# Two transformer stacks in one kernel: split activations moved to 448 bytes past a multiple of 512, one odd matmul in six stages, and three reorderings

## The chip, the cores and the metric

One Trainium2 chip, one of its cores. The time is the device time of one execution in microseconds (us). Five engines run side by side, each through its own list of instructions, and meet at semaphores: TensorE (PE: matmuls; PEld is its weight load), VectorE (DVE), ScalarE (ACT), GpSimd (POOL) and SyncE (SP, here the queue of the weight transfers).

## The reference

Input x is 256 tokens of 1024 features. It goes through an MLA layer and an mLSTM layer, each with a squared-ReLU MLP, then through a second stack: SwiGLU, short convolution, SwiGLU, and after a shared key/value projection SwiGLU, a sparse attention, SwiGLU. Cut to what the change touches:

```python
def rms_norm(x, g):
    y = x * lax.rsqrt(jnp.mean(x * x, axis=-1, keepdims=True) + EPS)
    return y * g

# MLA: 16 heads, 64 + 32 query/key features, 64 value features
cq = rms_norm(h @ w_dq, q_norm)
q = (cq @ w_uq).reshape(b, s, 16, 96)
dkv = h @ w_dkv
ckv = rms_norm(dkv[..., :256], kv_norm)
kv = (ckv @ w_ukv).reshape(b, s, 16, 64 + 64)
q, k = rms_norm(q, q_gain), rms_norm(k, k_gain)      # then rope on the last 32
o = softmax(q @ k.T * 96 ** -0.5, chunk mask) @ v
# mLSTM: 4 heads of 128 / 256, one row of decays per head
den = sum(qk); h = num / max(abs(den), exp(-m))
# MLPs and SwiGLU
x + square(relu(rms_norm(x, g) @ w1)) @ w2
x + (silu(gate) * up) @ w_out
```

## The kernel before

All matmuls of weights are made in three passes for precision. A weight tile `raw` of 128x1024 (512 KB) comes in by DMA into a ring of four; ScalarE rounds it to `w_hi` (`split`, L538), and VectorE or GpSimd subtracts to get the rest, `w_lo` (`take_lo`, L1006 on VectorE, L462 on GpSimd; `POOL_TILES` says which tiles GpSimd takes). Activations are split in the same way into a high and a low half that lie side by side: `xs` holds the layer's input, `os` attention outputs and the input of glu_2, `hs` the hidden features. A product of 128 features of weights with 256 tokens is then three matmuls of 256 columns: w_hi with x_hi, w_hi with x_lo, w_lo with x_hi (`narrow_product`, L1692, L1693, L1694). The `residual` stages, which read `hs`, use one matmul of 512 columns and one of 256. `token_major` stages (uk, uq, uv, mv, mo, kv, nq) hold the activations still and stream 512 columns of weights (L1820 to L1822).

`STAGES` is the order of the stages: name, tiles, outputs. Long stages that read `xs`: up_0 and up_1 (32 tiles each), glu_0, glu_1, glu_3 (44 each), cin (24). A tile of them is 24 matmuls. `feature` runs them: the first two tiles in pairs, with the row sums of the norm (`sums`) among the last of their products, then tile by tile, the last multiple of eight in a loop; `between` puts other work behind a tile.

Where things lie: each partition has `os` from byte 114112 (448 past a multiple of 512), `xs` from 130720 (160 past) and `hs` from 147104 (160 past). `bias` later takes the place of `os`, `w1c_all` that of `xs`, the `arena` that of `hs`. In the changed kernel `xs` and `w1c_all` begin at 130496 (448 past); the others stay.

Nothing is scheduled by a program: each engine's order is the order in which its part of the code is written. Of those orders the change touches four places:

- The start. ScalarE makes the high halves of x, splits tile 0, then squares x with splits 1 and 2 behind three squares each; VectorE makes the low halves, adds the squares into `ssq` (L1641) and takes the low tiles at the same places. TensorE warms up with 16 matmuls of ones, then runs tile 0, tile 1 (`sums` behind it), tile 2 of dq.
- MLA's projections. dkv and kr follow, and the latents go to `os` split (L1029 the low halves). `narrow` copies kr's output to `fsum` (L1048) for two transposes (`turn_narrow`) that stand behind the first half tile of uk. `sums("cq")` adds 5 blocks of squares for each of 2 token blocks (L1703) behind the second half tile. VectorE then evacuates uk, uq and uv (`up_kv`, L1234), each bank when its tiles are done; TensorE may start uq only when the first two banks of uk are read.
- MLA's heads. Per head: transposes, scores, maxima on VectorE, `exps` on ScalarE with `accum_out` for the row sums (L700), transposes of the probabilities, values (L1901 to L1903) and a scaling by the reciprocal of the sum.
- mLSTM. VectorE makes the decays by a scan, an add, a second scan (L1320 to L1322) behind the eight mqk outputs; TensorE turns the rows behind the third half tile of mv (`turn_rows`), and the scores, weights and numerators of the four heads follow between the half tiles of mv and mo. `head(h)` (L1364 to L1371) divides the numerators by the denominators.

## Time and profile before

| | us |
|---|---|
| median of 3 runs | 1621.61 |
| the runs | 1624.91, 1621.61, 1619.29 |
| profiled execution | 1625.26 |
| its span (first to last instruction) | 1623.4 |
| mean granted clock of TensorE | 0.986 of 2.4 GHz |

The profile is that of one execution. Busy times of matmuls overlap and their ends are modelled, so pace is read from starts or from counts in a stretch, to one matmul in either direction. A granted clock of 1.00 is 2.4 GHz, 0.50 is 1.2 GHz. "Idle before" and a wait tell how long an engine stood and what it waited for.

### The profile page before, as it was taken

The page shows a single profiled execution, that of the slowest core. Times are in us where ns is not written, and L with a number is a line of the kernel's source. Part 1 is how long each engine was busy: PE and PEld are TensorE (multiplying, and loading weights), DVE is VectorE, ACT ScalarE, POOL GpSimd, SP SyncE. Part 2 cuts the span into 40 slices and gives each one's busy share as a digit, 9 for nine tenths or more (in the row PEclk, how much of TensorE's full clock was granted, in tenths as well). Part 3 has the DMA queues.
Part 4 walks back from the last instruction along what each step waited for, and adds up shares of the span by engine and source line. Part 5 has one row for each costly group of instructions (what it writes and reads, how often), then busy time and mean ns, then how long its engine had stood idle before and what let it go on. Part 6 is the DMA issues. An engine that isn't in the chain of part 4 may idle for free.

```text
span 1623.4 us, 33219 instructions
## 1 busy us (share of the span) xinstructions
PE 1585.5 (98%) x11604; PEld 1492.1 (92%) x11604; DVE 1076.5 (66%) x1817; ACT 863.8 (53%) x1381; POOL 151.3 (9%) x133
## 2 busy tenths in 40 slices
PE   7899999999999999999999999999999999999999
PEld 6789998877999889999899999889999878999997
DVE  6668766645677666666787766678566755686665
ACT  5576554444765545445545545556455546664443
POOL 1650000075200000000000000000000032200000
PEclk8899999989999999999999999999999999999999
DMA  6226556543565565555655655556555871065564
GB/s 227 73 56 192 193 182 193 183 155 117 168 190 186 182 196 188 185 183 192 204 188 182 197 189 188 188 181 207 179 190 193 216 198 65 2 195 189 186 195 142
DMA packets 80766, 280.72 MB, mean 173 GB/s; under 512 B 8880, under 2 KB 12464, under 8 KB 80688
## 3 DMA queue, kind: packets, MB, share of 16 engines
q1 hardware_dynamic: 76800, 274.78, 52.5%
q10 hardware_dynamic: 3888, 4.85, 1.6%
q8 instruction: 54, 0.88, 0.2%
q14 instruction: 24, 0.20, 0.0%
HBM read 278.03 MB, written 1.57 MB: 172 GB/s over the span
## 4 chain that ended last, share of the span: by engine, by line
PE 90%; DVE 5%; ACT 2%; DMA 2%; issue 1%; DVEq 0%; ACTq 0%; SPq 0%
PE psum L1692 17%; PE psum L1693 17%; PE psum L1694 17%; PE psum L1684 16%; PE psum L1685 8%; PE psum L1820 2%; PE psum L1822 2%; PE psum L1821 2%; DMA raw<-tiles 1%; DVE w_lo L1006 1%; PE psum L2095 1%; PE psum L2046 1%; PE psum L1994 1%; ACT w_hi L538 1%; DVE w1c_all L1570 0%
## 5 line engine op out<-in xcount | busy, mean ns | idle before, releaser
L538 ACT ACTIVATE w_hi<-raw 128x1024 fp32r<-128x1024 f32 x518 | 546.8, 1057 | 447.9 <-PE psum L1694 263.2
L1006 DVE TENSOR_TENSOR w_lo<-raw,w_hi 128x1024 fp32r<-128x1024 f32 x472 | 577.0, 1223 | 219.6 <-ACT w_hi L538 219.2
L1692 PE MATMUL psum<-xs,w_hi 128*128 128x256 f32 x1928 | 541.6, 281 | 8.5 <-DVE w_lo L1006 5.8
L1694 PE MATMUL psum<-xs,w_lo 128*128 128x256 f32 x1928 | 539.9, 280 | 0.0
L1693 PE MATMUL psum<-xs,w_hi 128*128 128x256 f32 x1928 | 538.9, 279 | 0.0
L1684 PE MATMUL psum<-hs,w_hi 128*128 128x512 f32 x1216 | 421.9, 390 | 0.0
L1692 PEld LDWEIGHTS psum<-xs,w_hi 128*128 128x128 f32 x1928 | 363.5, 189 | 9.5 <-DVE w_lo L1006 6.2
L1693 PEld LDWEIGHTS psum<-xs,w_hi 128*128 128x128 f32 x1928 | 363.5, 189 | 0.3
L1694 PEld LDWEIGHTS psum<-xs,w_lo 128*128 128x128 f32 x1928 | 363.4, 188 | 0.0
L1685 PE MATMUL psum<-hs,w_lo 128*128 128x256 f32 x1216 | 342.9, 282 | 0.0
L1684 PEld LDWEIGHTS psum<-hs,w_hi 128*128 128x128 f32 x1216 | 228.3, 188 | 47.7
L1685 PEld LDWEIGHTS psum<-hs,w_lo 128*128 128x128 f32 x1216 | 229.8, 189 | 0.0
L462 POOL TENSOR_TENSOR w_lo<-raw,w_hi 128x1024 fp32r<-128x1024 f32 x46 | 110.8, 2419 | 1223.9 <-ACT w_hi L538 1191.5
L1692 PE MATMUL psum<-os,w_hi 128*128 128x256 f32 x544 | 152.9, 281 | 1.1 <-DVE os L1200 1.1
L1693 PE MATMUL psum<-os,w_hi 128*128 128x256 f32 x544 | 151.1, 278 | 0.0
L1694 PE MATMUL psum<-os,w_lo 128*128 128x256 f32 x544 | 151.0, 278 | 0.0
L1692 PEld LDWEIGHTS psum<-os,w_hi 128*128 128x128 f32 x544 | 102.2, 188 | 1.8 <-DVE os L1200 1.6
L1693 PEld LDWEIGHTS psum<-os,w_hi 128*128 128x128 f32 x544 | 102.2, 188 | 0.1
L1694 PEld LDWEIGHTS psum<-os,w_lo 128*128 128x128 f32 x544 | 102.0, 188 | 0.0
L1029 DVE SCALAR_TENSOR_TENSOR xs<-x,vec,xs 128x256 fp32r<-128x256 f32 (+1 forms) x80 | 38.1, 483 | 53.0 <-ACT xs L552 53.0
L1148 DVE TENSOR_TENSOR fsum<-psum,sil 128x256 f32<-128x256 f32 x88 | 37.3, 424 | 46.5 <-PE psum L1694 45.7
L552 ACT ACTIVATE xs<-x,vec (+1 forms) x80 | 40.1, 509 | 49.9 <-DVE x L1100 26.5
(285 smaller groups left out, 1571.5 us busy)
## 6 DMA issues: line engine op xcount, KB each, us to landing
raw<-tiles SPq DMA_DIRECT2D x518, 512.0 KB, 4.2
bias<-bias_dram ACTq DMA_DIRECT2D x8, 256.0 KB, 8.4
x<-x_in SPq DMA_DIRECT2D x4, 256.0 KB, 5.1
w1c_all<-w1c_k ACTq DMA_DIRECT2D x4, 256.0 KB, 4.2
w1c_all<-w1c_v ACTq DMA_DIRECT2D x4, 256.0 KB, 5.3
y_out<-x SPq DMA_DIRECT2D x8, 128.0 KB, 3.4
con<-consts SPq DMA_DIRECT2D x1, 771.0 KB, 8.9
bias_dram<-bias_row ACTq DMA_DIRECT2D x1, 512.0 KB, 7.2
```

What stands on the lines that cost most here:

```text
L462: pool.tensor_tensor(w_lo[s][:, :], raw[s][:, :], w_hi[s][:, :].bitcast(F32), ALU.subtract).then_inc(lo_ready, 1)
L538: act.activation(w_hi[s][:, :], raw[s][:, :], ACT.Copy).then_inc(hi_ready, 1)
L552: act.activation(dst, src, ACT.Copy, scale=gain).then_inc(xhi_ready, 1)
L1006: dve.tensor_tensor(w_lo[s][:, :], raw[s][:, :], hi_of(w_hi[s][:, :]), ALU.subtract).then_inc(lo_ready, 1)
L1029: dve.scalar_tensor_tensor(out=dst, in0=src, scalar=gain, in1=hi_of(hi), op0=ALU.mult, op1=ALU.subtract).then_inc(xs_ready, 1)
L1148: dve.tensor_tensor(f, bank(b, 0, S), sil[u // 2][:, :] if u % 2 else rb[:, :], ALU.mult).then_inc(out_read, 1)
L1684: pe.matmul(bank(out_bank), w_hi[s][:, c:c + P], src[:, chunk:chunk + 2 * S], start=first, stop=False)
L1685: return pe.matmul(bank(out_bank, 0, S), w_lo[s][:, c:c + P], src[:, chunk:chunk + S], start=False, stop=last)
L1692: pe.matmul(out, w_hi[s][:, c:c + P], x_hi, start=first, stop=False)
L1693: pe.matmul(out, w_hi[s][:, c:c + P], x_lo, start=False, stop=False)
L1694: return pe.matmul(out, w_lo[s][:, c:c + P], x_hi, start=False, stop=last)
L1820: pe.matmul(out, x_hi, w_hi[s][:, col:col + 512], start=c == 0, stop=False)
```

## The change

- Places: `apart_x` ahead of `xs` is dropped, `apart_h` of the same size stands behind `xs`. So `xs` (and `w1c_all`) lie 224 bytes lower.
- `odd_matmul`, one fp32 matmul of 60 columns whose result nobody reads, stands behind the fourth tile of up_0, up_1, glu_0, cin and glu_1, and behind the third of glu_3.
- Start: ScalarE's table is loaded ahead of the first input, tile 1 is split (high and low) before any square, tile 2 behind the fourth square and the fifth add; 24 instead of 16 warm-up matmuls.
- MLA: `narrow("kr")` ahead of the last three low halves; VectorE takes the low parts of the first two uq tiles, GpSimd begins with the third; VectorE adds the five blocks of squares to two before `sums("cq")`; gains, bias row and mask copies come ahead of `norm("cq")`; the sums for the head norms are spread among the evacuations; the values carry a column of ones (65 instead of 64 per head), so the third matmul gives the row sums, `accum_out` goes, and the output of a head is one reciprocal and one multiplication; the Exp table is loaded ahead and one split stands behind the first heads; eight fp32 matmuls of ones stand ahead of the first transposes of probabilities.
- mLSTM: VectorE takes the low tiles during mqk (GpSimd begins behind mv's first ones), the decays and the second scan stand behind the fifth and sixth mqk output; the causal mask is an operand of the minimum ahead of the exponential instead of two multiplications behind it; `head` has two small operations instead of three; rows and scores come one or two half tiles earlier.

The diff, cut to its core:

```diff
-        sb("apart_x", [P, 56])
         with nc.sbuf_tensor("w1c_all", [P, 2 * 16 * P], F32) as w1c_all:
             pass
         xs = sb("xs", [P, KD * 2 * S], F32R)
+        sb("apart_h", [P, 56])
...
-        POOL_TILES = [(TILE0["uq"], TILE0["wo_a"] + RING), (TILE0["mgate"] + RING, TILE0["wo_m"] + RING), (TILE0["ngate"] + RING, TILE0["wo_n"] + RING)]
+        POOL_TILES = [(TILE0["uq"] + 2, TILE0["wo_a"] + RING), (TILE0["mv"] + RING, TILE0["wo_m"] + RING), (TILE0["ngate"] + RING, TILE0["wo_n"] + RING)]
...
-                                       bias=nmx[u][:, tb:tb + 1], accum_out=rsum[u][:, tb:tb + 1]).then_inc(a_exp, 1)
+                                       bias=nmx[u][:, tb:tb + 1]).then_inc(a_exp, 1)
...
+            act.preload_act_table(ACT.Copy)
...
+            split(1)
             for k in range(KD):
-                if k in (3, 6):
-                    split(k // 3)
+                if k == 4:
+                    split(2)
...
+                dve.wait_ge(sq_ready, SQ0["cq"] + 1)
+                first, second = (ASQ[:, 0:2 * KQ * S].rearrange("p (k s) -> p k s", s=KQ * S)[:, :, n * S:(n + 1) * S] for n in range(2))
+                then(dve.tensor_tensor(first, first, second, ALU.add))
+                dve.tensor_tensor(ASQ[:, 0:S], ASQ[:, 0:S], ASQ[:, 2 * S:3 * S], ALU.add).then_inc(cq_added, 1)
+                for t in range(TILE0["uq"], TILE0["uq"] + 2):
+                    take_lo(t)
...
                 def outputs(i, u):
-                    dve.wait_ge(a_exp, i * 8 + 2 * (u + 1))
-                    then(dve.reciprocal(rinv[u], rsum[u]))
+
                     dve.wait_ge(a_pv, i * 4 + (u + 1))
...
+                    then(dve.reciprocal(rinv[u].unsqueeze(2), pv[:, :, VD:VD + 1]))
...
+                plain("mqk", 8, lambda o: m_qk[:, o * S:(o + 1) * S], lo=True, between={4: decays, 5: stabilizers})
...
-                    dve.tensor_tensor(w[:, 0:P], w[:, 0:P], causal, ALU.mult)
-                    then(dve.tensor_tensor(w[:, S:S + P], w[:, S:S + P], causal, ALU.mult))
...
-                    then(dve.tensor_tensor(m_dn[h], m_dn[h], floor, ALU.max))
+                    then(dve.scalar_tensor_tensor(out=m_nd[h], in0=den, scalar=-1.0, in1=floor, op0=ALU.mult, op1=ALU.max))
+                    then(dve.scalar_tensor_tensor(out=m_dn[h], in0=den, scalar=1.0, in1=m_nd[h], op0=ALU.mult, op1=ALU.max))
...
+            def odd_matmul():
+
+                pe.matmul(bank(7, 64, 124), const("blockdiag", 0, P), ones[:, 0:60], start=True, stop=True)
...
-            warm(16)
+            warm(24)
...
-            feature("up_0", FF1, "ffn_0", norm_="ffn_0")
+            feature("up_0", FF1, "ffn_0", norm_="ffn_0", between={3: odd_matmul})
...
-            feature("glu_3", 2 * FF2, "post_1", norm_="post_1")
+            feature("glu_3", 2 * FF2, "post_1", norm_="post_1", between={2: odd_matmul})
```

VectorE's order between MLA's low halves (`os`) and the reciprocal of `norm("cq")`, before:

```order
22 L1029 SCALAR_TENSOR_TENSOR os<-arena,vec,os 128x256 [waits xhi_ready] x2
23 L1006 TENSOR_TENSOR w_lo<-raw,w_hi 128x1024 [waits hi_ready]
24 L1029 SCALAR_TENSOR_TENSOR os<-arena,vec,os 128x256 [waits xhi_ready] x3
25 L1048 COPY fsum<-psum 32x256 [waits tile_done]
26 L1022 RECIPROCAL rstd<-std 128x4 [waits std_ready]
27 L1215 TENSOR_SCALAR bias_row<-psum 16x512 [waits row_ready,dve_step]
28 L1219 COPY arena<-con 2x512 [waits loaded]
```

The same place on VectorE now:

```order
22 L1012 TENSOR_TENSOR w_lo<-raw,w_hi 128x1024 [waits hi_ready]
23 L1056 COPY fsum<-psum 32x256 [waits tile_done]
24 L1035 SCALAR_TENSOR_TENSOR os<-arena,vec,os 128x256 [waits xhi_ready] x3
25 L1223 TENSOR_TENSOR arena<-arena 128x2x256 [waits sq_ready]
26 L1224 TENSOR_TENSOR arena<-arena 128x256 [waits dve_step]
27 L1012 TENSOR_TENSOR w_lo<-raw,w_hi 128x1024 [waits hi_ready] x2
28 L1228 TENSOR_TENSOR row<-row 128x64 [waits loaded]
29 L1230 TENSOR_SCALAR bias_row<-psum 16x512 [waits row_ready,dve_step]
30 L1233 COPY arena<-con 2x512 x2
31 L1234 MEMSET arena 128x32
32 L1028 RECIPROCAL rstd<-std 128x4 [waits std_ready]
```

The copy to `fsum` went ahead of three low halves; two adds, two low tiles, the bias row and the mask copies went ahead of the reciprocal.

VectorE's order from mLSTM's eight mqk outputs to the copy of the turned rows, before:

```order
315 L1040 TENSOR_TENSOR arena<-psum,rb 128x256 [waits tile_done] x8
316 L1317 MEMSET arena 4x256
317 L1320 SCALAR_TENSOR_TENSOR arena<-arena 4x256 [waits m_tanh,dve_step]
318 L1321 SCALAR_TENSOR_TENSOR arena<-arena 4x256 [waits dve_step]
319 L1322 SCALAR_TENSOR_TENSOR arena<-arena 4x256 [waits dve_step]
320 L1323 TENSOR_SCALAR arena<-arena 4x256 [waits dve_step]
321 L1324 TENSOR_TENSOR arena<-arena 4x256
322 L1329 COPY arena<-psum 128x16 [waits m_at]
```

The same stretch on VectorE now, from the fifth mqk output on:

```order
311 L1046 TENSOR_TENSOR arena<-psum,rb 128x256 [waits tile_done]
312 L1012 TENSOR_TENSOR w_lo<-raw,w_hi 128x1024 [waits hi_ready]
313 L1347 SCALAR_TENSOR_TENSOR arena<-arena 4x256 [waits m_tanh]
314 L1348 SCALAR_TENSOR_TENSOR arena<-arena 4x256 [waits dve_step]
315 L1046 TENSOR_TENSOR arena<-psum,rb 128x256 [waits tile_done,dve_step]
316 L1012 TENSOR_TENSOR w_lo<-raw,w_hi 128x1024 [waits hi_ready]
317 L1352 SCALAR_TENSOR_TENSOR arena<-arena 4x256
318 L1353 TENSOR_SCALAR arena<-arena 4x256 [waits dve_step]
319 L1354 TENSOR_TENSOR arena<-arena 4x256
320 L1046 TENSOR_TENSOR arena<-psum,rb 128x256 [waits tile_done]
321 L1012 TENSOR_TENSOR w_lo<-raw,w_hi 128x1024 [waits hi_ready]
```

The first scan and the add stand between outputs five and six, the second scan (a SCALAR_TENSOR_TENSOR here too) between six and seven, each output with a low tile behind it.

## Rows read from the trace of the kernel before

**Rows 1.** The page: span, and busy time (share of the span) and instructions by engine.
```profile
span 1623.4 us, 33219 instructions
PE 1585.5 (98%) x11604; PEld 1492.1 (92%) x11604; DVE 1076.5 (66%) x1817; ACT 863.8 (53%) x1381; POOL 151.3 (9%) x133
```
**Rows 2.** Stretches, matmuls of L1692 alone: stretch, length, busy (count), clock, DMA, GB/s.
```profile
150.00:220.00 70.00, 55.83 (x201) 1.00 0.61 200
422.00:438.00 16.00, 12.97 (x48) 1.00 0.53 182
660.00:730.00 70.00, 55.48 (x199) 1.00 0.55 185
920.00:1010.00 90.00, 71.78 (x258) 1.00 0.56 187
1180.00:1240.00 60.00, 48.71 (x177) 1.00 0.60 191
```
**Rows 3.** Timeline of PE in glu_2: start, duration, line, out<-in, columns, count.
```profile
1174.80 0.28 PE L1693 MATMUL psum<-os,w_hi 128*128 128x256 f32 x1
1174.92 0.28 PE L1694 MATMUL psum<-os,w_lo 128*128 128x256 f32 x1
1175.04 0.33 PE L2006 MATMUL psum<-arena,con 128*128 128x60 f32 x2
1175.18 0.36 PE L1692 MATMUL psum<-os,w_hi 128*128 128x256 f32 x1
1175.38 0.28 PE L1693 MATMUL psum<-os,w_hi 128*128 128x256 f32 x1
1175.49 0.28 PE L1694 MATMUL psum<-os,w_lo 128*128 128x256 f32 x1
```
**Rows 4.** Waits of PE: line, waited for, us in total, times, longest.
```profile
PE psum L1925 <- DVE arena L1324: 3.8, 1, 3.8
PE psum L1835 <- DVE fsum L1048: 3.2, 1, 3.2
...
PE psum L1952 <- DVE arena L1371: 2.1, 1, 2.1
```
**Rows 5.** Stretches: length, busy PE, PEld, DVE, ACT, POOL; then clock, DMA, GB/s.
```profile
15.40:20.70 5.30, 5.25 (x24) 5.25 (x25) 3.79 (x6) 1.81 (x2) 0.00 (x0) 0.50 0.56 193
...
39.50:53.20 13.70, 12.69 (x41) 10.38 (x41) 6.07 (x9) 2.42 (x4) 2.71 (x2) 0.53 0.22 73
...
353.50:363.80 10.30, 9.62 (x27) 6.99 (x28) 1.53 (x5) 1.06 (x1) 2.35 (x1) 0.54 0.30 95
...
391.00:394.50 3.50, 3.50 (x11) 2.81 (x10) 0.99 (x5) 0.00 (x0) 0.00 (x0) 0.61 0.32 123
```
**Rows 6.** Timeline of DVE, start of the kernel.
```profile
12.25 2.01 DVE L1641 TENSOR_TENSOR ssq<-ssq,arena 128x256 f32<-128x256 f32 x4
14.18 1.22 DVE L1006 TENSOR_TENSOR w_lo<-raw,w_hi 128x1024 fp32r<-128x1024 f32 x1
```
**Rows 7.** Timeline of DVE, MLA projections.
```profile
33.31 5.49 DVE L1029 SCALAR_TENSOR_TENSOR os<-arena,vec,os 128x256 fp32r<-128x256 f32 x3
...
47.92 2.94 DVE L1219 COPY arena<-con 2x512 f32<-2x512 f32 x2
```
**Rows 8.** Timeline of PE, first matmul of uq.
```profile
52.85 0.47 PE L1820 MATMUL psum<-w_hi,os 128*128 128x512 f32 x1 [1.01 <-issue]
```
**Rows 9.** Timeline of POOL, MLA projections.
```profile
33.53 4.98 POOL L462 TENSOR_TENSOR w_lo<-raw,w_hi 128x1024 fp32r<-128x1024 f32 x2 [32.39 <-DVE w_lo L1006]
```
**Rows 10.** Groups of ACT in MLA's heads, 80 to 106 us.
```profile
L700 ACT ACTIVATION_READ_ACCUMULATOR arena<-psum,arena,rstd 128x1 f32 x24 | 4.8, 202 | 0.0
```
**Rows 11.** Timeline of DVE, mLSTM's rows.
```profile
348.28 2.45 DVE L1321 SCALAR_TENSOR_TENSOR arena<-arena 4x256 f32<-4x256 f32 x1
350.76 2.71 DVE L1322 TENSOR_TENSOR_SCAN arena<-arena 4x256 f32<-4x256 f32 x1
```
**Rows 12.** Timeline of DVE, mLSTM's first head.
```profile
387.34 1.90 DVE L1368 TENSOR_TENSOR arena<-arena 128x2 f32<-128x2 f32 x1
```

More of the change, by code:

```diff
@@ L288, in build @@
         qkT = [part(14272 + 512 * j, 512) for j in range(2)]
-        mx, nmx, rsum, rinv = ([part(15296 + 8 * j + 2 * u, TB) for u in range(4)] for j in range(4))
+        mx, nmx, rinv = ([part(15296 + 8 * j + 2 * u, TB) for u in range(4)] for j in range(3))
         turn_bank, score_bank = ([(OUT0["uv"] + j + k) % 4 for k in range(2)] for j in (0, 2))
@@ L1042, in plain @@
                         take_lo(TILE0[name] + o + RING)
+                    if between and o in between:
+                        between[o]()
             def narrow(name, width):
@@ L1243, in mla @@
                 up_kv("uk", k_tok, 1)
-                then(dve.tensor_tensor(gq[:, 0:NOPE], gq[:, 0:NOPE], gk[:, 0:NOPE], ALU.mult))
+                head_sums(0)
                 up_kv("uq", q_tok, 0)
-                for n in range(3):
+                for n in (1, 2):
                     head_sums(n)
@@ L1307, in mlstm @@
             def mlstm():
+                causal = const("causal", 0, P)
+                then(dve.memset(m_mask, 0.0))
+                dve.tensor_scalar(m_mask[:, 0:P], causal, -1.0, 1.0e30, ALU.add, ALU.mult)
                 for o, (dst, b) in enumerate(((m_ti, "b_i"), (m_tf, "b_f"))):
@@ L1698, in sums @@
                 if name == "cq":
-                    pe.wait_ge(sq_ready, SQ0["cq"] + 1)
+                    pe.wait_ge(cq_added, 1)
                     for tb in range(TB):
-                        for k in range(KQ + KKV):
-                            col, first, last = (4, 0, KQ - 1) if k < KQ else (6, KQ, KQ + KKV - 1)
+                        for k, col in ((0, 4), (KQ, 6)):
                             ins = pe.matmul(bank(STAT, col + tb, col + tb + 1), ASQ[:, k * S + tb * P:k * S + (tb + 1) * P], ones[:, 0:1],
-                                            start=k == first, stop=k == last)
+                                            start=True, stop=True)
                 else:
```

102 lines of the change are left out of this document (57 added, 45 removed).

## The prediction

> **What bounds the kernel now.** I read the page first. TensorE is busy 98% of a span of 1623.4 us [rows 1]: what matters is how fast its matmuls follow each other, and the few places where it stands or runs at its lower clock. So I took three views: counts of one matmul line in long stretches (pace), TensorE's waits, and stretches with their granted clock.
>
> **Pace.** L1692 is the first of the three 256-column matmuls of a product, so a stretch divided by three times its count is the start-to-start time of one. From [rows 2]: 70 us / (3 x 201) = 116.1 ns in up_0, 90 / (3 x 258) = 116.3 ns in glu_1, 70 / (3 x 199) = 117.3 ns in glu_0, all from `xs` (160 bytes past a multiple of 512); and 60 / (3 x 177) = 113.0 ns in the last two thirds of glu_2, which reads `os` (448 past). The reader is to see that `os` is not always fast. Just before the single 60-column matmul at 1175.04 the products of glu_2 start at 1174.80 and 1174.92; behind it at 1175.38 and 1175.49 [rows 3]. The step from 0.12 to 0.11 us is small, but it stays so for the rest of the stage: the 113.0 ns begin here. I therefore read three paces: a slow one of about 117.5 at either place, and a quick one whose price depends on the place, 116.2 at 160 bytes and 113.0 at 448.
>
> **Waits and clock.** TensorE waits 3.2 us for the `fsum` copy, 3.8 us for the rows of the mLSTM and 2.1 us for the first head's values [rows 4], and at the start for the second tile's `w_lo`, which begins at 14.18 us [rows 6]. Behind each such gap a stretch at 1.2 GHz follows: 15.4 to 20.7 us (clock 0.50), 39.5 to 53.2 (0.53), 353.5 to 363.8 (0.54), 391 to 394.5 (0.61) [rows 5]. Each costs about half its length where TensorE has work. These gaps, not throughput, are what the three repairs touch.
>
> **The change part by part.** All against the profiled execution, 1625.3 us; the median of the three runs is 3.7 us lower, and I take that off at the end.
>
> *Start.* Now VectorE holds the second tile's `w_lo` (14.18 us) behind four sums of squares of 0.50 us each that began at 12.25 [rows 6]. After, it comes straight behind the `xs` remainders, about 2.7 us earlier, so tile 1 runs from about 12.7 at full clock, 2.8 us instead of 5.3. But the row sums that follow tile 1 then wait: VectorE has one memset, eight adds (8 x 0.50) and a split (1.22) behind the second `w_lo`, to about 18.2 where the sums stood at 20.7. Gain 2.5 us; ends 0 (a new 2.7 us wait brings the low clock again) and 5.3 (nothing waits). The eight more warm-up matmuls (some 1.8 us at full clock) end before the first tile is ready and cost nothing. The table load moved ahead is inside the same 2.5.
>
> *MLA projections.* From the end of `kr` (33.4) to the first matmul of uq (52.85) there are now 19.4 us [rows 8]. Two of three remainders on VectorE take 2.5 us each instead of 0.5, 5.49 in all, while GpSimd works on two `w_lo` for 4.98 us [rows 9]; the copy for the transposes comes behind them [rows 7]. After, the copy stands ahead of the three, VectorE takes the two tiles itself, and the sums need 8 instead of 20 records. TensorE's own work there is then, as an estimate, 24 matmuls of 512 columns at twice 116 ns, 5.6 us, and some 2 us for the bias row, the transposes and the sums: 7.6 us. VectorE's chain to the first evacuations of uk is longer. What it does there today, nine instructions from reciprocal to evacuation, is 6.07 us busy [rows 5], of which 2.1 is the second L1219 copy's wait (2.94 us for the two [rows 7], 0.4 each without): 3.9 us. Ahead of that come the small copy 0.4, three remainders at 0.5, two adds of 512 and 256 elements (0.50 for 256 [rows 6], so some 1.1 in all) and two splits of 1.22 [rows 6]: 9.3 us together. One thing is late next: GpSimd (2.5 us a tile [rows 9]) starts on its first tile just as VectorE comes to the two L1219 copies, and one or both wait again. I take 10.5 us, ends 9.3 and 13. Then 19.4 - 10.5 = 8.9; TensorE waits 2 to 5 us there, so a stretch of low clock may follow (the shortest and the startup one in [rows 5] are 3.5 and 5.3 us long, half of that lost). I take 8 us, ends 4 and 10.1.
>
> The Trainium skill states in "GPSIMD Engine Reference", section "Specifications", that GpSimd shares its SBUF interfaces with VectorE and that instructions with two SBUF inputs, or in a two-port mode, contend. The trace agrees (2.5 us in place of 0.5 for the remainders [rows 7]); by it both copies would wait for GpSimd and the term would be 6 us in place of 8.
>
> *Heads.* Dropping `accum_out` takes two accumulator reads of 202 ns per head from ScalarE [rows 10], of which some 0.2 us lie on its path. TensorE goes through three value matmuls of 65 instead of 128 columns; a 60-column one occupies 0.14 us (1175.04 to 1175.18 [rows 3]) and I estimate 0.07 less per matmul than for 128, from the 0.12 us that 256 columns of the split products take. Both engines are full in the loop, so about 0.2 us per head, 16 heads: 3.2 us. The first head starts about 1 us earlier, as the second-to-last reductions no longer stand behind the evacuation and the Exp table is loaded ahead. Together 4 us, ends 1 and 6.
>
> *mLSTM.* Scan, add and scan took 2.45 and 2.71 us in their last two pieces under GpSimd [rows 11], while TensorE waited 3.8 us [rows 4]. After, they are done between the fifth and seventh mqk tile, with GpSimd idle, since VectorE takes those tiles: per tile 0.42 + 1.22 us against 2.8 us of TensorE, so 8 x 1.15 us are free for about 4 us of scans. Nothing is late there. Gain 3.8 plus half of the 9.62 busy us at 0.54 [rows 5]: 8.6 us. At the first head's values an L1368 of 1.90 us goes [rows 12] (two small operations that read PSUM replace three), and with it the 2.1 us wait and 1.7 us of low clock: 3.6 us. Together 12.2, ends 7 and 13.
>
> *Pace of the long stages.* up_0, up_1, glu_0, glu_1, glu_3 and cin have 32 + 32 + 44 x 3 + 24 = 220 tiles of 24 matmuls from `xs`. With the odd matmul behind tile 4 (3 in glu_3), some 197 tiles or 4728 matmuls go from 116.2 to 113.0 if it does there what the one at 1175.04 did: 15.1 us, and 1 us more for glu_0. Against it, the first tiles may go at 117.5 (+0.6), and each odd matmul adds about 0.22 us (0.34 from its start to the second product, less one interval [rows 3]), six of them 1.3. I take 14 us. The other end: all 5280 at 117.5, 5.5 us lost with the odd ones 6.8. The bound on the gain is 17.
>
> The Trainium skill gives in "TensorE: Matmul & The Clock Gate", section "Wait — 56ns, not 53.3ns?", a warm start-to-start time of N / 2.4 GHz + about 2.5 ns, so 109.2 ns for 256 columns, with no word of an address. The counts stand 4 to 8 ns above [rows 2], so the trace does not bear it out; by it this term would be 0.
>
> **Sum.** 2.5 + 8 + 4 + 12.2 + 14 = 40.7 us. 1625.3 - 40.7 = 1584.6, less 3.7: **1581 us**.
>
> **Rivals.**
> *The place does not matter in `xs`.* What is quick in glu_2 would belong to that stage and its history. For it: only one stage shows the flip; against: wo_m reads `os` as well and has 48 in 16 us, 111 to 113 ns [rows 2]. Pace term 0: 1595.
> *Slow pace.* At 448 bytes the stages fall into the slow state and the odd matmul only helps in some, since it needs the state that glu_2 had. For it: before 1175 glu_2 ran slow at 448, and glu_0 shows that stages of the same code differ. None quick: 1581 + 14 + 6.8 = 1602; half of the tiles: about 1590.
> *The repairs half fail.* The new waits of 2.7 and 2 to 5 us bring the low clock back twice and the copies wait for GpSimd: lower ends, 0 + 4 + 1 + 7 = 12 in place of 26.7: 1596.
> *Slower than before.* Reading `xs` at 448 collides with what ScalarE and VectorE write in these stages, at a pace that glu_2 did not show. With the repairs at 26.7 us it takes (26.7 - 1.3) / 5280 = 4.8 ns more per matmul, 121 ns, to cancel them; at 122.5 the result is 1621.6 + 8 = 1630. No stretch of [rows 2] shows more than 117.3.
>
> **How the numbers follow.** Forecast as summed (at least five of the six stages quick): 0.42, from 1573 to 1587. Part of the stages quick, near 1590: 0.25. Slow pace, near 1602: 0.12. Place without effect, near 1595: 0.08. Repairs half: 0.10. Slower: 0.03. The range that should hold 8 in 10 is 1572 to 1602. A measurement of this kernel can tell about 0.3%, 4.9 us, from no change: faster 0.94, same 0.02, slower 0.04.
>
> **What the changed profile would show.** Start: the second `w_lo` before 13 us and row sums near 18. MLA: no wait at the transposes of `kr`, uq from about 42 us. Heads: no accumulator reads, each head 0.2 us shorter. mLSTM: no wait at the transposes of the rows, clock 1.00 in the whole stage. Pace: 60 us stretches of glu_1 and up_0 with 177 counts, not 172 or 170. I would be wrong first of all by counts of 170 behind the odd matmul, then by a clock of 0.5 anywhere ahead of 60 us.

## The result and the profile after

| | before | after |
|---|---|---|
| median, us (four runs each) | 1622.09 | 1599.47 |
| the runs | 1619.29 to 1624.91 | 1598.62 to 1602.94 |
| profiled execution | 1625.26 | 1602.94 |

The ratio is 0.9865, with a 95% interval of 0.9842 to 0.9887. The change makes the kernel 22.6 us faster, 1.4%; 40.7 were forecast.

The page of the changed kernel, span and TensorE's busy time, against [rows 1]:

```profile
span 1601.2 us, 33207 instructions
PE 1580.1 (99%) x11636; PEld 1490.4 (93%) x11636; DVE 1065.1 (67%) x1806; ACT 862.7 (54%) x1349; POOL 121.8 (8%) x121
```

**Where the time went.** The start of the same piece of work in both traces, read from TensorE's timelines (each stretch ends at the time given, in us, and begins where the one above it ends):

| stretch | before | after | gained |
|---|---|---|---|
| start, to the first matmul of uk | 34.33 | 33.52 | 0.8 |
| MLA projections, to uq | 52.85 | 41.62 | 10.4 |
| heads and wo_a, to the row sums of up_0 | 142.79 | 132.01 | -0.4 |
| up_0, to down_0 | 227.92 | 215.19 | 2.0 |
| down_0, mLSTM, to wo_m | 415.53 | 391.72 | 11.1 |
| wo_m and up_1, to down_1 | 529.41 | 503.44 | 2.1 |
| down_1 to out_0 (glu_0) | 743.37 | 717.62 | -0.2 |
| out_0, cin, cout to the sums of glu_1 | 899.76 | 874.88 | -0.9 |
| glu_1, to out_1 | 1018.49 | 994.96 | -1.3 |
| kv and glu_2, to out_2 | 1251.42 | 1229.28 | -1.4 |
| sparse attention, to wo_n | 1411.07 | 1387.43 | 1.5 |
| wo_n and glu_3, to out_3 | 1558.27 | 1536.04 | -1.4 |

The three reorderings gained 22 us (0.8 + 10.4 - 0.4 + 11.1), the whole of what the change brought. The two up stages gained 4.1, the glu, cin and kv stretches lost 5.2: the pace part came out at nothing. The sparse attention brought 1.5 more.

**Pace.** Counts of the first matmul of a product (L1722 now) in stretches of 60 us of up_0, up_1, glu_0, glu_1, glu_2, glu_3, to be held against [rows 2]:

```profile
150.00:210.00 60.00, 48.74 (x177) 33.05 (x177) 1.00 0.65 194
440.00:500.00 60.00, 48.72 (x177) 33.10 (x177) 1.00 0.63 193
620.00:680.00 60.00, 47.53 (x171) 31.89 (x170) 1.00 0.59 187
900.00:960.00 60.00, 47.53 (x171) 31.85 (x170) 1.00 0.59 186
1160.00:1220.00 60.00, 47.58 (x170) 31.84 (x171) 1.00 0.58 189
1440.00:1500.00 60.00, 47.54 (x170) 31.84 (x171) 1.00 0.57 185
```

177 counts are 113 ns per matmul, 170 or 171 are 117.3. The up stages are quick; glu_0, glu_1 and glu_3 are slow behind their odd matmul, and so is glu_2, which was quick before. From here on I use the mean distance of starts over a whole stretch, which is finer than a count. A count takes in the matmuls that reach over the ends of its stretch, so it comes out some 0.3 to 0.6 ns low: the kernel before goes at 116.7, 117.8 and 113.3 where the prediction read 116.2, 117.3 and 113.0. In the long stages this distance takes three values only, 113.3 and 117.8 ns at 448 bytes, 116.7 (seldom 117.8) at 160.

The odd matmul (L1747) in up_0 and in glu_0, timeline of TensorE:

```profile
138.81 0.33 PE L1747 MATMUL psum<-ones,con 128*128 128x60 f32 x2
138.94 0.36 PE L1722 MATMUL psum<-xs,w_hi 128*128 128x256 f32 x1
139.14 0.28 PE L1723 MATMUL psum<-xs,w_hi 128*128 128x256 f32 x1
139.26 0.28 PE L1724 MATMUL psum<-xs,w_lo 128*128 128x256 f32 x1
139.37 0.28 PE L1722 MATMUL psum<-xs,w_hi 128*128 128x256 f32 x1
```
```profile
604.33 0.33 PE L1747 MATMUL psum<-ones,con 128*128 128x60 f32 x2
604.47 0.36 PE L1722 MATMUL psum<-xs,w_hi 128*128 128x256 f32 x1
604.67 0.28 PE L1723 MATMUL psum<-xs,w_hi 128*128 128x256 f32 x1
604.79 0.28 PE L1724 MATMUL psum<-xs,w_lo 128*128 128x256 f32 x1
604.90 0.28 PE L1722 MATMUL psum<-xs,w_hi 128*128 128x256 f32 x1
```

The same instructions; from the start of the odd matmul to the fourth product behind it 0.56 us in the first case and 0.57 in the second. The rows hardly show it; the counts of the stage behind them do.

**Waits and clock.** TensorE's longest waits, and stretches with their granted clock, to be held against [rows 4, 5]:

```profile
PE psum L1739 <- DVE ssq L1671: 2.5, 1, 2.5
PE psum L2074 <- DVE arena L1599: 2.2, 1, 2.2
```
```profile
16.00:19.80 3.80, 1.34 (x8) 1.12 (x7) 3.50 (x6) 1.50 (x2) 0.00 (x0) 0.92 0.53 177
19.80:22.70 2.90, 2.90 (x14) 2.90 (x15) 1.92 (x2) 2.52 (x4) 0.00 (x0) 0.52 0.62 216
98.40:100.60 2.20, 1.54 (x6) 1.35 (x6) 0.46 (x2) 0.03 (x1) 0.00 (x0) 0.50 0.29 117
100.60:104.60 4.00, 3.92 (x17) 3.52 (x18) 1.28 (x3) 1.41 (x4) 0.00 (x0) 0.51 0.00 0
330.00:391.00 61.00, 60.58 (x280) 47.72 (x280) 21.48 (x53) 30.44 (x48) 33.74 (x15) 1.00 0.44 145
```

The mLSTM's two low stretches are gone. At the start the row sums (L1739) wait 2.5 us and 2.9 us at 1.2 GHz follow. A low stretch that the kernel before did not have stands at the end of MLA's heads, 98.4 to 104.6 us.

**MLA projections.** VectorE, GpSimd and TensorE, three timelines, the answer to [rows 7 to 9]:

```profile
35.25 2.36 DVE L1012 TENSOR_TENSOR w_lo<-raw,w_hi 128x1024 fp32r<-128x1024 f32 x2
...
38.48 0.76 DVE L1233 COPY arena<-con 2x512 f32<-2x512 f32 x2
```
```profile
39.38 2.37 POOL L465 TENSOR_TENSOR w_lo<-raw,w_hi 128x1024 fp32r<-128x1024 f32 x1 [38.23 <-ACT w_hi L541]
```
```profile
41.62 0.47 PE L1853 MATMUL psum<-w_hi,os 128*128 128x512 f32 x1 [0.93 <-issue]
```

The two copies take 0.76 us (2.94 before) and end at 39.24, 0.14 us before GpSimd begins. uq begins 9.1 us behind the end of kr (32.56), against 19.5 before, and the granted clock is 1.00 from 22.7 to 97 us.

### The profile page after: what moved, and what is told of

The parts are those of the page before. It is cut to its first block, busy times and chain, and to the rows that moved or that the text cites. A ratio compares the mean times of both kernels' runs of the same rounds, so it can differ in the third digit from the quotient of the medians.

```text
span 1601.2 us, 33207 instructions
## 1 busy us (share of the span) xinstructions
PE 1580.1 (99%) x11636; PEld 1490.4 (93%) x11636; DVE 1065.1 (67%) x1806; ACT 862.7 (54%) x1349; POOL 121.8 (8%) x121
## 4 chain that ended last, share of the span: by engine, by line
PE 93%; DVE 4%; ACT 1%; issue 1%; DMA 0%; SPq 0%; DVEq 0%; ACTq 0%
PE psum L1722 18%; PE psum L1724 18%; PE psum L1723 18%; PE psum L1714 17%; PE psum L1715 9%; PE psum L1853 2%; PE psum L1854 2%; PE psum L1855 2%; PE psum L2129 1%; PE psum L2080 1%; PE psum L2113 1%; PE psum L2028 1%; DMA raw<-tiles 0%; DVE w_lo L1012 0%; PE psum L1917 0%
## 5 line engine op out<-in xcount | busy, mean ns | idle before, releaser
L1012 DVE TENSOR_TENSOR w_lo<-raw,w_hi 128x1024 fp32r<-128x1024 f32 x484 | 591.9, 1223 | 225.5 <-ACT w_hi L541 224.8
L1722 PE MATMUL psum<-xs,w_hi 128*128 128x256 f32 x1928 | 540.9, 281 | 2.2 <-DVE w_lo L1012 1.5
L1722 PEld LDWEIGHTS psum<-xs,w_hi 128*128 128x128 f32 x1928 | 362.6, 188 | 3.1 <-DVE w_lo L1012 1.7
L465 POOL TENSOR_TENSOR w_lo<-raw,w_hi 128x1024 fp32r<-128x1024 f32 x34 | 81.3, 2395 | 1230.7 <-ACT w_hi L541 1230.7
L1722 PE MATMUL psum<-os,w_hi 128*128 128x256 f32 x544 | 154.2, 284 | 0.7 <-DVE os L1208 0.6
L1722 PEld LDWEIGHTS psum<-os,w_hi 128*128 128x128 f32 x544 | 102.5, 188 | 1.5 <-DVE os L1208 1.4
```

The lines of the kernel that those rows point to most:

```text
L465: pool.tensor_tensor(w_lo[s][:, :], raw[s][:, :], w_hi[s][:, :].bitcast(F32), ALU.subtract).then_inc(lo_ready, 1)
L1012: dve.tensor_tensor(w_lo[s][:, :], raw[s][:, :], hi_of(w_hi[s][:, :]), ALU.subtract).then_inc(lo_ready, 1)
L1722: pe.matmul(out, w_hi[s][:, c:c + P], x_hi, start=first, stop=False)
```

## The experiments

Each verdict is a ratio to the kernel before on the same chip; the medians of before lay between 1616.8 and 1618.9 us there.

### Which part brought what

```diff
-            feature("up_0", FF1, "ffn_0", norm_="ffn_0", between={3: odd_matmul})
+            feature("up_0", FF1, "ffn_0", norm_="ffn_0")
...
```


> The changed kernel (1599.5 us) without the six odd matmuls; `xs` stays at 448 bytes. In the changed kernel only up_0 and up_1 turned quick (113.3 ns per matmul), right behind the odd one, all other long stages go at 117.8. Theory A (the odd matmul turns a stage from slow to quick, where it meets the right moment; the place alone never does): up_0 and up_1 at 117.8 to their ends, 2 x 28 tiles x 24 x 4.5 ns = 6.0 us more, six odd matmuls of 0.22 us less: 1599.5 + 4.7 = 1604. Rival B (the place alone is what makes them quick, the odd matmul is idle): no stage changes its pace, 1598.

Measured 1607.49 us, ratio 0.9928 (0.9901 to 0.9955). Up_0 and up_1 stay at 117.8 throughout, and every long stage with them. Theory A: the place alone did not make a long stage quick. An odd matmul is not the only thing that does: wo_a and wo_m, which read `os` at 448, go at 113.3 in this kernel, which has none anywhere. Of the 3.5 us above its 1604 the profiled executions show 3.1 in the sparse attention (see below), but also up_0's row sums 3.2 us earlier, so the difference is not fully placed.

`repairs` is that kernel with `xs` moved back:

```diff
+        sb("apart_x", [P, 56])
         with nc.sbuf_tensor("w1c_all", [P, 2 * 16 * P], F32) as w1c_all:
             pass
         xs = sb("xs", [P, KD * 2 * S], F32R)
-        sb("apart_h", [P, 56])
```


> The changed kernel with `xs` back at 160 bytes and without the odd matmuls: the three reorderings alone. Theory A (reorderings gave 24 of the 22.6 us, place and odd matmul together gave nothing: 6 us won in up_0 and up_1 against the state of before are eaten by cin, glu_1 and glu_3 going at 117.8 instead of 116.7 and by glu_2): cin, glu_1, glu_3 at 116.7 again, 1622.1 - 24 = 1598, no slower than the changed kernel. Rival B (the pace part brought its 14 us and the reorderings only 9): 1613.

Measured 1597.58, ratio 0.9858 (0.9822 to 0.9893), where the whole change has 0.9865. The reorderings are all of the gain. The stages that read `xs` go at 116.7, and glu_2 turned quick at the same 60-column matmul as before.

`pace_only` is the kernel before with `xs` moved and the six odd matmuls:

> The kernel before with `xs` at 448 bytes and the six odd matmuls, without the reorderings. Theory A (which stage turns quick depends on the moment at which the odd matmul comes, and the two kernels reach it by different histories): some of the six stages quick, not necessarily up_0 and up_1; each quick one of 44 tiles gives 3.4 us against 116.7, each slow one costs 1.1: between 1609 (all) and 1627 (none). Rival B (the odd matmul works in up stages and never in glu and cin): up_0 and up_1 quick, the rest slow, 1622 + 0 to 3. Rival C (my forecast's term): 1608.

Measured 1617.75, ratio 0.9999 (0.9976 to 1.0022). Of the six stages up_1 alone turned quick, where the changed kernel had up_0 too. The code of the stage does not decide it: `two_odd` has the same instructions as the changed kernel up to up_0, and there up_0's odd matmul missed. In the six kernels with one 60-column odd matmul at these places or ahead of any other (the changed one, pace_only, two_odd, res_probe, start_tail, best1) the first one took 11 of 36 stages to quick.

### What an odd matmul does

```diff
+                for cols in (60, 52, 60) if shape == 1 else (60,):
+                    for shift in range(0, 128, 8):
+                        odd_matmul(cols)
+                        for k in range(12 if shape == 1 else 6):
+                            w = w_hi[s][:, k % 6 * P:(k % 6 + 1) * P]
+                            if shape == 1:
+                                pe.matmul(bank(7, 0, S), w, xs[:, S + shift:2 * S + shift], start=True, stop=True)
...
+            feature("glu_0", 2 * FF2, "pre_0", norm_="pre_0", between=behind({u: (60, 1) for u in range(3, 20)}))
```


> The changed kernel with measurements put in; the added matmuls write a PSUM bank that nobody reads, and its total time says nothing. In up_0, behind tile 4: for each of 16 places (every 32 bytes within 512) an odd matmul and 12 products of 256 columns from `xs`, three times over, then the same for pairs of 512 and 256 columns and for 512 columns of `w_hi`. In up_1 and glu_0 an odd matmul of 60 columns behind each of 12 and 17 tiles, in glu_1 and glu_3 other widths and two or three in a row behind 15 tiles each. Theory A (two states; the quick one's price depends on the place of the moving operand): pitches of 117.8 at every place in the slow state, in the quick one a value that depends on the place, 113.3 at 448 and 116.7 at 160, and other places as good as 448; the odd matmul throws the stage from one state to the other by chance of its moment, so that among 29 odd ones of 60 columns both directions occur. Rival B (the odd matmul always ends in the same state of a stage): up_1 quick behind all 12, glu_0 slow behind all 17.

Two things came out. First the place: mean distance of starts in ns of the last ten of twelve 256-column matmuls, three tries each (the least and the most of the three):

| bytes past a multiple of 512 | 64 | 160 | 192 | 320 | 416 | 448 | the other ten |
|---|---|---|---|---|---|---|---|
| least | 113.3 | 116.7 | 117.6 | 113.3 | 116.7 | 113.3 | 117.2 to 119.6 |
| most | 117.8 | 117.3 | 117.8 | 117.8 | 117.3 | 117.8 | 118.0 to 119.9 |

Timeline of TensorE at 128 bytes and at 64: from the first of the twelve to the odd matmul behind them 1.51 and 1.45 us.

```profile
146.63 1.68 PE L1766 MATMUL psum<-xs,w_hi 128*128 128x256 f32 x12
148.14 0.32 PE L1748 MATMUL psum<-ones,con 128*128 128x60 f32 x2
```
```profile
169.66 1.62 PE L1766 MATMUL psum<-xs,w_hi 128*128 128x256 f32 x12
171.11 0.32 PE L1748 MATMUL psum<-ones,con 128*128 128x52 f32 x2
```

Second the toggling: in up_1 the odd matmul behind every tile made the stage quick, slow, quick, slow, twelve times; in glu_0 the first missed and the other sixteen alternated. From quick, all 25 single ones of any width from 16 to 120 columns ended the quick pace. From slow, 26 of 26 hit where the product before took 118 or 119 ns, and 0 of 5 where it took 116 or 117 (the 24 of 28 in the next expectation is a miscount; and in the other kernels six with 118 missed, so this one distance is not a full sign). Where another came a tile behind a miss, it hit each time.

What does sort the cases are the recorded durations of the last three products ahead of the odd matmul, to the nanosecond. In all fourteen traces together, for single fp32 ones of 32 to 128 columns in a slow stretch at 448 bytes, they are 280 (once 281), 279 and 279 ahead of each of the 95 hits, and 279, 279, 277 or 279, 280, 279 ahead of each of the 64 misses. The slow pace repeats over three matmuls (280, 279, 279 through all of glu_0 in the changed kernel), and a tile is 24 of them, so a stage stays in its phase: one phase of the three is turned to quick. Which phase a stage begins in differs between kernels with the same code ahead of it, and why was not found.

An odd matmul that breaks the quick pace in up_1:

```profile
570.42 0.33 PE L1748 MATMUL psum<-ones,con 128*128 128x60 f32 x2
570.55 0.37 PE L1722 MATMUL psum<-xs,w_hi 128*128 128x256 f32 x1
570.76 0.28 PE L1723 MATMUL psum<-xs,w_hi 128*128 128x256 f32 x1
```

Rival B falls: the stage does not decide, what the odd matmul meets does. This also explains glu_2 of the changed kernel: its own matmuls at 1144 us had made it quick, and L2040 at 1149.90, the very one that had made it quick before, broke it.

```diff
-            feature("glu_0", 2 * FF2, "pre_0", norm_="pre_0", between={3: odd_matmul})
+            feature("glu_0", 2 * FF2, "pre_0", norm_="pre_0", between={3: odd_matmul, 4: odd_matmul})
...
```


> The changed kernel with a second odd matmul one tile behind the first in glu_0, cin, glu_1 and glu_3, and one in glu_2, a tile behind its own 60-column matmul (L2040). In the measuring kernel the odd matmul took a stage from slow to quick in 24 of the 28 cases in which the last product before it took 118 or 119 ns, and never where it took 116 or 117; behind a miss the next one, a tile later, hit. Theory A (the slow pace has a rhythm of three and a miss moves the stage to the next step of it): all five stages quick behind the second; 39 + 19 + 39 + 40 tiles and 27 in glu_2, 164 x 24 x 4.5 ns = 17.7 us, less 5 x 0.22: 1599.5 - 16.6 = 1583. Rival B (the moment of a stage is set by something that differs from run to run): some of the five quick, and a spread between runs of several us: 1587 to 1600.

Measured 1590.74, ratio 0.9821 (0.9803 to 0.9840): faster than the changed kernel, but not by 17. Glu_0, cin and glu_3 missed first and hit with the second; glu_2 hit; glu_1 hit with the first, and the second broke it; up_0, with one only, missed. Two odd ones need a miss first, so no fixed number of them is right for every run. The profile fits theory A's rhythm of three; what it left out is that the second one breaks what the first has turned.

```diff
+                    else:
+                        pe.matmul(bank(7, 0, n), w_hi[next_slot[0]][:, 0:P], xs[:, 0:n], start=True, stop=True)
```


> A measuring kernel; the added matmuls write a PSUM bank that nobody reads. In up_1, glu_0, cin, glu_1 and glu_3 of the changed kernel a matmul of some kind and, a tile later, the 60-column odd one, three times for each of 20 kinds: 256-byte-place matmuls of the split type of 32 to 512 columns, two of 128, fp32 ones of 256 and 128 columns, two of 60. Theory A (the stage has a few fixed rhythms, one of them quick, and a matmul of another length shifts it from one to another): some kinds leave the quick rhythm quick (those whose own length fits), others always end it, each kind the same way each time. With such a kind a stage could be brought to quick from any of its rhythms. Rival B (any foreign matmul ends the quick rhythm): no kind keeps it.

One kind kept the quick pace, in the one case in which it met it: two matmuls of 128 columns of the split type. Timeline of TensorE in glu_3; from the last product ahead of them to the second product behind it is 0.45 us, four times 113.3:

```profile
1437.67 0.28 PE L1724 MATMUL psum<-xs,w_lo 128*128 128x256 f32 x1
1437.78 0.33 PE L1753 MATMUL psum<-xs,w_hi 128*128 128x128 f32 x2
1437.95 0.33 PE L1722 MATMUL psum<-xs,w_hi 128*128 128x256 f32 x1
1438.12 0.28 PE L1723 MATMUL psum<-xs,w_hi 128*128 128x256 f32 x1
```

Single ones of 32 to 192, 224 and 320 columns ended it each time they met it; the other widths met only slow stages, so for these nothing is shown. The kernel `kick` uses the pair:

```diff
+            def kick(t, src=xs, b=7):
+
+                pe.wait_ge(lo_ready, t + 1)
+                for _ in range(2):
+                    pe.matmul(bank(b, 0, P), w_hi[t % RING][:, 0:P], src[:, 0:P], start=True, stop=True)
...
+            feature("up_0", FF1, "ffn_0", norm_="ffn_0", between=kicks("up_0", 2, 3))
```


> The kernel best1 with another foreign matmul in place of the odd one: two matmuls of 128 columns of the split type (w_hi of the next tile with `xs`), behind the third and again behind the fourth tile of the six long stages, and behind tiles 20 and 21 of glu_2. In probe2 it was the one kind among those met in the quick rhythm (113.3 ns) that left it quick (from the last quick product to the second behind it 453 ns = 4 x 113.3), and it took a slow stage to quick as the odd one does. Theory A (each of the two either takes a stage a step on or leaves it quick): all seven stages at 113.3 from the fourth or fifth tile on; against the reorderings alone (1597.6) 196 tiles x 24 x 3.4 ns = 16.0 us less, 3 for start and heads less, 14 x 0.23 = 3.2 more: 1582, and the runs closer together than those of best1 (1585.5 to 1595.1). Rival B (it was one chance case): one to four stages slow, as with the odd ones, 1586 to 1592.

Measured 1584.34, ratio 0.9801 (0.9785 to 0.9816), five runs from 1583.6 to 1587.5. All seven stages are quick; the count of L1722 in glu_1:

```profile
900.00:960.00 60.00, 48.73 (x177) 33.09 (x177) 1.00 0.58 193
```

In three of the seven the first pair hit and the second found it quick and left it so; in four the first missed and the second hit. The same sign as above sorts them: over all traces the pair hit in the 19 cases with 280, 279, 279 and in none of the 11 others.

The same kernel with `xs` moved back, by the same two lines as in `repairs`:

> The kernel `kick` (1584.3 us, ratio 0.980) with `xs` back at 160 bytes, nothing else. Theory A (the quick rhythm's price is set by the place of the moving operand: 113.3 at 448, 116.7 at 160, as the probe had it at 448, 64 and 320 against 160 and 416): the six stages that read `xs` at 116.7 at best, 196 tiles x 24 x 3.4 ns = 16 us more, 1600; if the pair of matmuls leaves some at 117.8, up to 1605. glu_2, which reads `os` at 448, at 113.3 as before. Rival B (the pair of matmuls alone makes the pace, and the place does nothing): 113.3 in all six, 1584.

Measured 1601.57, ratio 0.9897 (0.9878 to 0.9917). The same stretch has 172:

```profile
900.00:960.00 60.00, 47.83 (x172) 32.27 (x172) 1.00 0.55 186
```

The medians are 17 us apart. In the two profiled executions the six stages that read `xs` differ by 15.6, which is what the place is worth where the quick pace is held; glu_2 adds 4.3, since in this run both of its pairs missed (117.8 from 1165 us on). That is the one miss in 19 stages at 448 bytes; the pair is much surer than the odd matmul, not sure. At 160 bytes the pairs had nothing to do: the six stages went at 116.7 before the first one already, and stayed there.

### The residual stages

```diff
-                                ins = product(b, (t % RING, k * P), c, src, c == 0, c == chunks - 1)
+                                ins = narrow_product(b, (t % RING, k * P), c, src, c == 0, c == chunks - 1)
...
-        sb("apart_h", [P, 56])
```


> The kernel two_odd with `hs` at 448 bytes too, and the residual stages (down_0, down_1, out_0 to out_3), so far a 512 and a 256 column matmul in 346.7 ns, made of three 256-column ones; an odd matmul behind each of their first three outputs. ScalarE's copy of the second half and VectorE's addition of the halves go. Theory A (what is quick is the 256-column matmul at this place, wherever it stands): stretches of 113.3 in the residual stages, 340 ns a product against 346.7; in the quick state 1216 x 6.7 ns = 8 us less, in the slow one 1216 x 6.7 more. Rival B (the rhythm of `xs` stages does not exist there): always 117.8.

One run, 1601.66. Stretches of 113.3 stand in all six residual stages, and down_0 began quick, since up_0 had ended so: the border did not end the pace, the odd matmul at 227.1 did. Theory A. `best2` puts it all together:

```diff
+                    if o < 4:
+                        kick(t0 + o + 1, src)
...
+                        if name == "ngate" and k == KD - 1:
+                            warm(3, 6)
```


> The kernel `kick` with more of the same: `hs` at 448 bytes and the residual stages made of three 256-column matmuls (ScalarE's copy and VectorE's addition of the halves go), the pair of 128-column matmuls also behind two tiles of wo_a, wo_m, wo_n, cout and mqk, and fillers of 3 and 4 matmuls of ones in the two waits of ngate, where in some runs the clock fell and in others not (best1: 0.74 between 1290 and 1300 us, two_odd: 1.00). Theory A (the quick rhythm lasts over the border of two stages, since nothing foreign stands there): residual stages at 113.3 without a matmul of their own, 1216 x 6.7 ns = 8.1 us less; wo_a, wo_n and mqk 2 us less; ngate 0 to 3 us less: 1570. Rival B (the border or the loop of a residual stage ends the rhythm): six residual stages at 117.8, 1216 x 3 x 2.2 = 8 us more in place of 8 less, 1587.

Measured 1575.59, ratio 0.9734 (0.9719 to 0.9749). The count in down_0, out_0 and glu_1, each product now three matmuls (L1719 is the third):

```profile
235.00:295.00 60.00, 48.73 (x177) 33.12 (x177) 1.00 0.59 192
740.00:770.00 30.00, 24.37 (x89) 16.56 (x89) 1.00 0.63 208
900.00:960.00 60.00, 48.67 (x178) 33.18 (x177) 1.00 0.60 192
```

Every residual stage is quick without a matmul of its own, and the six together took 8.3 us less than in `kick`, for 8.1 expected. The median is still 5.6 us above the 1570 of theory A. The fillers in ngate did not do what they were for: from ngate to wo_n the clock was still 0.91 in the profiled execution, the slowest of the six.

### The start, the heads, and GpSimd

```diff
-                feature("dq", 3, "mix_0", norm_="mix_0", norm_at=1)
+                feature("dq", 3, "mix_0", norm_="mix_0", norm_at=2)
...
+                           lambda i, u: warm(2, turn_bank[0]) if isinstance(i, int) and i == H // 4 - 1 else None)
```


> The changed kernel with two things. Start: the row sums stand behind the third tile of dq, not the second, so that TensorE works while VectorE ends its adds. Heads: two matmuls of ones behind each transposes of probabilities of the last four heads, where TensorE waits for ScalarE. Theory A (my start term failed since the wait of 2.5 us ahead of the sums brought 1.2 GHz for 2.9 us, and my heads term since the clock fell between 98.4 and 104.5 us): no stretch at 0.5 at 20 us, end of kr 2.5 us earlier (30.1 for 32.6); no stretch at 0.5 behind 98 us, from the last head's values to the first full product of wo_a 1.2 us less. Rival B (low clock at these places is set by something before them): same low stretches at the same work, end of kr at 32, nothing gained in the heads.

One run, 1610.34. Both low stretches went: 16 to 23 us and 98 to 107.8 us now have a clock of 1.00, and kr ended at 30.34. At the heads the low stretch stands in all seven profiled executions without the fillers and in none of the five with them. At the start it is less clear: five of the seven with the old order had it, but `no_odd` and `probe` had the same wait of 2.4 us and a clock of 1.00 behind it (first matmul of uk at 31.2 and 31.4, here 31.3); none of the five with the new order had it. The gain was lost at once. Timelines of GpSimd, VectorE and TensorE:

```profile
37.16 2.38 POOL L465 TENSOR_TENSOR w_lo<-raw,w_hi 128x1024 fp32r<-128x1024 f32 x1 [36.02 <-ACT w_hi L541]
39.71 2.34 POOL L465 TENSOR_TENSOR w_lo<-raw,w_hi 128x1024 fp32r<-128x1024 f32 x1 [0.17 <-ACT w_hi L541]
```
```profile
37.19 5.15 DVE L1233 COPY arena<-con 2x512 f32<-2x512 f32 x2
```
```profile
44.71 0.77 PE L1853 MATMUL psum<-w_hi,os 128*128 128x512 f32 x1 [6.23 <-issue]
```

GpSimd began 0.03 us ahead of the copies, and each copy ended behind one of its two tiles: 5.15 us in place of 0.76, and uq at 44.71 in place of 41.62. The Trainium skill says in "SBUF — State Buffer", section "SBUF: two separate sides", that the port pair which GpSimd shares with a VectorE instruction in a two-port mode or with two SBUF inputs is an exclusive lock for the whole instruction, and whoever starts second waits in full. The trace agrees to 0.3 us: the copies end at 42.34, GpSimd's second tile at 42.05.

An early TensorE did not do this. GpSimd begins 5.86 us behind the first matmul of uk in `no_odd`, in the changed kernel and here alike; VectorE came to the copies 0.93 us later against it here (5.89 us, 4.96 in the other two).

`best1` is two_odd with both edits and the copies moved ahead of the two low tiles:

```diff
+                dve.wait_ge(loaded, 16 * 3)
+                at_ = CONST["onehot"]
+                for j in range(2):
+                    dve.tensor_copy(qkT[j][QK:QK + TB, :], con[QK:QK + TB, at_:at_ + 2 * S]).then_inc(a_mask, 1)
                 for t in range(TILE0["uq"], TILE0["uq"] + 2):
                     take_lo(t)
```


> The kernel two_odd (1590.7 us, ratio 0.982) with the start and the fillers in the last heads of start_tail, and with VectorE's two mask copies (L1233) moved ahead of the two low tiles. In start_tail GpSimd began its `w_lo` at 37.16 us, 0.03 us ahead of the copies, which then took 5.15 us for 0.76, and TensorE stood 6.2 us; in the changed kernel the copies ended 0.14 us before GpSimd began. Theory A (the gain of the start was lost there and nowhere else): copies 0.8 us wherever the start puts GpSimd, uq at 39.4 us where the changed kernel has 41.6, the heads 1 us less; 1590.7 - 3.2 = 1587.5. Rival B (the copies are hit at their new place too, or another of VectorE's steps is, such as the bias row): a step of over 2 us between 34 and 43 us and 1593.

Measured 1589.89, ratio 0.9821 (0.9795 to 0.9847). The copies take 0.76 again, uq begins at 40.48 (1.7 us of it a new wait for GpSimd's tile), the first product of wo_a comes at 100.22, for 101.80 in two_odd. So 1.6 us are left of the 3.2 expected, and its runs (1585.5 to 1595.1) spread too far to show them. The spread has a second source besides the pace: the sparse attention, from ngate to wo_n, the same code in each. Stretches of two_odd and of best1:

```profile
1284.72:1377.15 92.43, 88.10 (x665) 77.16 (x663) 53.94 (x234) 55.35 (x129) 32.56 (x30) 1.00 0.22 74
```
```profile
1282.70:1383.66 100.96, 95.97 (x664) 83.68 (x663) 53.86 (x234) 55.47 (x129) 32.53 (x30) 0.92 0.25 70
```

92.4 us at full clock, 101.0 at 0.92; the kernel before has 98.6, the changed one 97.1, no_odd 100.3. Its waits of 0.8, 0.9 and 2.2 us are the same in two_odd (clock 1.00) and in the changed kernel (0.95); whether the clock falls behind them differs from one profiled kernel to the next. Why was not settled.

## Why the prediction was right, and where it was wrong

The median, 1599.5, lies in the range (1572 to 1602) and on the side forecast, but 18 us from the likeliest value, near the upper end: the range held because the rivals had stretched it, not because the sum was right. It came out beside the rival called slow pace (1602, given 0.12), and the mechanism is that rival's as well, stages slow at 448 bytes and an odd matmul that helps in some. That the number agrees so closely is partly luck, since the reorderings brought 22 us and not the 26.7 that the rival keeps.

- *Start*, 2.5 forecast, 0.8 measured. The second `w_lo` is at 11.90 (forecast: before 13) and the sums at 18.6 (near 18), as said. The step that failed is the size: behind the new wait, named as the lower end, came 2.9 us at 1.2 GHz. Where they stayed away with the same wait (no_odd), the first matmul of uk came at 31.2 in place of 33.5, 2.3 us earlier, and in start_tail at 31.3. The 0.8 is one draw: over seven kernels with this start that matmul came between 31.2 and 34.2.
- *MLA projections*, 8 forecast, 10.4 measured, just above the end of 10.1. No low clock followed the waits, and the copies escaped GpSimd by 0.14 us. For the forecast that was luck, though it does not change from run to run (0.13 to 0.15 us in all seven kernels with this order): the mechanism that I named (GpSimd starts as VectorE comes to the copies) is real, and start_tail paid 4.4 us for it.
- *Heads*, 4 forecast, -0.4 measured. Timeline of TensorE, the value matmuls of one head, before (128 columns) and after (65):

```profile
81.33 0.39 PE L1901 MATMUL psum<-arena 128*128 128x128 f32 x2
81.55 0.39 PE L1902 MATMUL psum<-arena 128*128 128x128 f32 x2
81.78 0.39 PE L1903 MATMUL psum<-arena 128*128 128x128 f32 x2
```
```profile
71.39 0.33 PE L1934 MATMUL psum<-arena 128*128 128x65 f32 x2
71.56 0.39 PE L1935 MATMUL psum<-arena 128*128 128x65 f32 x2
71.78 0.39 PE L1936 MATMUL psum<-arena 128*128 128x65 f32 x2
```

  The starts are 0.22 us apart in both but for the first step, 0.17: half the columns save 0.05 us there, not 0.2. The step that failed is the scaling of time with columns, from one row of 60 columns in glu_2 with a product of another kind behind it. Here the weight loads (PEld) of L1935 and L1936 are 0.22 us apart with either width, which fits that they set the pace; no run tests it. A head takes 2.11 us on TensorE before and 2.04 after, so the accumulator reads that left ScalarE brought nothing that can be seen. 1.4 us came in all (from first to last head 31.9 and 31.2, the first head 0.7 earlier), and the low clock at 98.4 took more than it back: start_tail with fillers has 7.5 us from the last head's first value matmul to wo_a's undisturbed products, the changed kernel 9.4, the kernel before 7.6.
- *mLSTM*, 12.2 forecast, 11.1 measured for down_0 to wo_m, where the slower pace of mgate and mqk (117.8 ns for 116.7) took some 0.2. Its clock is 1.00 throughout. Right by its own steps.
- *Pace*, 14 forecast, 0.3 measured in the six stages and -1.1 with glu_2. The step that failed is "if it does there what the one at 1175.04 did". I had one case of a flip and made a rule of it. The runs put in its place: the odd matmul turns a slow stage in one phase of three (11 of 36 stages), breaks those already quick, and a stage at 448 bytes that is not quick goes at 117.8, 1.1 ns slower than at 160, where the row sums mostly leave 116.7. The step on the place was right: 113.3 at 448 and not at 160, in `xs` as in `os` (kick against kick_160). The term itself was sound as a possible gain: in the six stages kick, its pairs included, is 12.9 us quicker than repairs in the profiled executions.
- *Not forecast*: 1.5 us in the sparse attention, within its own spread of 8.6 us over the kernels, and 1.4 lost in glu_2, a stage that the change does not touch and that I took as given.

## What to carry to other kernels

A pace that differs between stages of the same code is a hidden state; before building on an instruction that once changed it, put that instruction behind every tile of a stage and see what it does from each state. One measuring kernel showed in one run what the sum had wrong. Sort the outcomes by what stood just ahead of each one, and by more than one number of it: here the last three durations told what the last distance alone did not. Look for the disturbance that leaves the good state alone, not for the one that happened to reach it.

When an edit shifts one engine against another, list which shared resource it now meets: GpSimd beginning 0.14 us behind the end of the copies or 0.03 us ahead of their start decided between 0.76 and 5.15 us. The cure is to move the short instruction to where the other engine has nothing to start.

Count a narrower matmul's gain from start-to-start times in its own place: here 65 columns for 128 left two steps of three at 0.22 us.

## What the runs showed of the hardware

- The start-to-start time of a 256-column matmul of the split type at full clock depends on the place of its moving operand within 512 bytes and on a state that lasted until a foreign matmul came: 113.3 or 117.8 ns at 448, 64 and 320; 116.7 to 117.3 at 160 and 416 (117.8 through glu_0 of the kernel before, at 160); up to 119.9 at 224 and 480. The slow pace at 448 has a rhythm of three matmuls, and its phase told in all 159 cases whether an fp32 matmul turned it. What the state is, was not found.
- The state passes over loops and stage borders; 168 us (up_0 from its second pair on, down_0 and the first products of mgate, in best2) went in it with no other matmul between. An fp32 matmul of 16 to 120 columns ended it in all 25 cases of the measuring kernel.
- Three matmuls of 256 columns (340 ns) at 448 bytes in the quick state are quicker than one of 512 and one of 256 (346.7, at 160 bytes).
- A VectorE copy between two SBUF tensors waited for the GpSimd subtraction that had begun before it, 5.15 us for two copies in place of 0.76; VectorE's scaling from PSUM took 0.68 us under a GpSimd subtraction (L1256, changed kernel) and 0.69 without one (start_tail).
